# First expert gathered on TensorE, last normed rows stored from ScalarE, two tiles of the last stage summed by TensorE

## The chip, the cores and the metric

One Trainium2 chip, one of its cores; the program runs on that core alone. The metric is device time in microseconds (us), the median of several executions, lower is better. The core has TensorE (PE), VectorE (DVE), ScalarE (ACT), GpSimd (POOL) and SyncE (SP), each with its own instruction stream, and 16 DMA engines that all queues share. Engines wait for one another through semaphores only.

## What is computed

The block has one layer, 512 tokens of width 1024, all in float32. Two mixers, a gated merge and a cross-attention add to the residual `x`; the part that matters here comes after them:

```python
h = rmsnorm(x, norm_ffn_g)                      # 512 x 1024
group_prob = softmax(h @ w_group_router + b_group_router)      # 4 groups
gp, gi = top_k(group_prob, 1)
in_group = logits of the 8 experts of group gi  # h @ w_expert_router + b
ew, ei = top_k(softmax(in_group), 2)            # two experts per token
weights = gp * ew / sum(ew)
for e in range(32):
    hid = silu(h @ w_exp_gate[e]) * (h @ w_exp_up[e])     # 1024 -> 256
    out += combine[:, e] * (hid @ w_exp_down[e])          # 256 -> 1024
x = x + out
return rmsnorm(x, norm_final_g)
```

Each expert has 3 MB of weights, 96 MB in all.

## The kernel before

The tokens lie in four tiles (`NT = 4`) of 128 rows; the residual is `xres[:, t, :]`. Up to the router the work is a list of jobs that `job_order` (L126) writes out by hand; every engine walks the same list and does its part of each job. TensorE does the job and increments `done`, then the engine that `emptied_by` (L205) names reads the job's PSUM bank. Banks are given in turn, eight of them (L290 to L301). The jobs that end the list:

- `("co", t, n)`: half n of the cross-attention's output rows of tile t. VectorE adds it to `xres` (L1865). After n = 1 ScalarE squares the row to get its sum (L1545) and GpSimd makes the inverse root in six small operations (L870 to L875, `ffn_rstd`).
- `("hT", "ffn", t, q)`: TensorE transposes four blocks of `xres` (L1024), ScalarE copies them to `x_turned` (L1548). It waits until both halves of `co` are added.
- `("rt", t)`: router logits, 8 sums (L977 through `sums`), then a chain of some fifteen small operations on VectorE (L1872 to L1888) that picks the two experts. ScalarE makes the normed row `x_row[t]` (L1552, recorded at L1360), and GpSimd, after its own three operations (L880, L882), stores it to `h_rows` in device memory (L884).
- `("pos", t)`: the place of each token within its expert, as two one-hot tables `at_slot` of 128 tokens by 64 slots (L1891, L1894).
- `("ls",)`: the list of rows for each expert, by 32 matmuls (L1269), read by VectorE at L1896 to L1898 (`idx_ready`); `("most",)`: the largest count.

The order of these jobs for the last tile is at L183 and L184.

The expert stage comes next. `UNROLL = 6` sets of weights lie in SBUF, the sixth in the place of the ring. The first six experts are loaded ahead: SP issues five parts of 1 MB and the final norm's gain row after the last `co` job (L747 to L752). From expert 6 on, `load_expert` (L754) loads gate and up when the gate_up of the expert six before is done (L761), and down when its down is done (L763). GpSimd gathers an expert's rows from `h_rows` (L902), after all four stores have landed and the list is there (L886 to L888); up to three gathers are ahead. TensorE turns the rows (L1292), VectorE multiplies them by the norm's gains into `xgT` (L1926), TensorE does gate_up (L1305), then the turn of the next expert, then the hidden layer's transpose (L1326) and down (L1315). ScalarE copies the result (L1569) and GpSimd scatters it to `y_half` (L907). All engines run the 32 experts as a loop over six at a time; on TensorE and VectorE the loop starts at expert 0.

The last stage: after all scatters SP loads the two results of each token (L786, eight loads of 0.5 MB), VectorE adds them to `xres` with their weights, tile by tile (L1955), ScalarE squares (L1593), VectorE makes the inverse root by a shift and three Newton steps (`rms`, L1616). Tiles 0 and 1 are scaled by ScalarE (L1597) and multiplied by the gain row on GpSimd (L967), tiles 2 and 3 by VectorE (L1965). SP stores each tile (L789).

Of the kernel before, what the change touches and what calls it, by code (L numbers as in the profile page):

```python
# [33 lines left out]
P = 128  # L34
# [91 lines left out]
def job_order():  # L126
# [56 lines left out]
    jobs += [("co", 3, 0), ("rt", 2), ("pos", 1), ("co", 3, 1), ("pos", 2), ("hT", "ffn", 3, 0), ("hT", "ffn", 3, 1), ("rt", 3), ("pos", 3)]  # L183
    jobs += [("ls",), ("most",)]  # L184
# [5 lines left out]
PARTIAL = ("gp", "wp")  # L190
# [14 lines left out]
def emptied_by(job):  # L205

    if job[0] in PARTIAL:
        return None
    return "act" if job[0] in ON_ACT or job[:2] == ("hT", "ffn") else "dve"

# [31 lines left out]
def program(nc, x, mem, rel_bias_table, norm_mix_g, w_in, a_sink, b_conv_w, b_A_log, b_dt_bias, b_norm_g,  # L242
# [48 lines left out]
    for n, job in enumerate(jobs):  # L291
        gates = at["gp", 0, 0] <= n <= at["ga", 7]
        if job[0] in ("gp", "ga"):
            bank_index[job] = BANKS - 1
        elif job[0] == "wo":
            bank_index[job] = bank_index["wp", job[1], job[2]]
        else:
            turn_no = (turn_no + 1) % (BANKS - 1 if gates else BANKS)
            bank_index[job] = turn_no
        before_in_bank[job] = held.get(bank_index[job])  # L300
        held[bank_index[job]] = job  # L301
# [6 lines left out]
    with ExitStack() as ctx:  # L308
# [82 lines left out]
        prob = [r.rearrange("p (h m) -> p h m", h=X_HEADS) for r in x_row]  # L391
        x_turned = [r.rearrange("p (k t) -> p k t", k=KD) for r in x_row]
# [48 lines left out]
        at_slot = [cut(NT * CAP, "p (t s) -> p t s", t=NT) for _ in range(2)]  # L441
        dest_of = [cut(NT * EXPERTS, "p (t e) -> p t e", t=NT) for _ in range(2)]
# [36 lines left out]
        hrow_out = [sem("hrow_out0"), sem("hrow_out1")]  # L479
# [35 lines left out]
        put_set, y_in = sem("put_set"), [sem(f"y_in{t}") for t in range(NT)]  # L515

        more_w, more_idx_in, more_idx, more_gathered = sem("more_w"), sem("more_idx_in"), sem("more_idx"), sem("more_gathered")
        more_turned, more_turned_sb, more_gu, more_gth = sem("more_turned"), sem("more_turned_sb"), sem("more_gu"), sem("more_gth")
        more_gated, more_hid, more_hidT, more_hidT_sb = sem("more_gated"), sem("more_hid"), sem("more_hidT"), sem("more_hidT_sb")
        more_down, more_y, more_out = sem("more_down"), sem("more_y"), sem("more_out")  # L520
        fin_ready, out_done = sem("fin_ready"), sem("out_done")
        scale_ready, scaled, early_fin = sem("scale_ready"), sem("scaled"), sem("early_fin")
# [126 lines left out]

        def y_total(b):  # L650
# [40 lines left out]
        def _(sp):  # L691
# [60 lines left out]
            sp.dma_start(gain_out, norm_final_g.rearrange("(o d) -> o d", o=1).to_broadcast([P, D])).then_inc(gains_in, 16)  # L752
# [18 lines left out]
            with sp.If(most > CAP):  # L771
# [8 lines left out]
                sp.wait_ge(more_out, 16 * MORE)  # L780
            for b in range(DEEP):
# [5 lines left out]
            for t in range(NT):  # L787
                sp.wait_ge(*((early_fin, t + 1) if t < 2 else (fin_ready, t - 1)))
# [5 lines left out]
        def _(pool):  # L794
# [28 lines left out]
            for job in jobs:  # L823
# [42 lines left out]
                if k == "co" and c == 1:  # L866
# [8 lines left out]
                    after(pool.tensor_tensor(y, y, y2, ALU.mult), ffn_rstd)  # L875
                if k == "rt":
# [6 lines left out]
                    pool.wait_ge(hrow_ready, c + 1)  # L883
                    pool.dma_start(h_rows[c * P:(c + 1) * P, :], x_row[c]).then_inc(hrow_out[c % 2], 16)  # L884
# [11 lines left out]
            def gather(i, b):  # L896
# [3 lines left out]
                pool.wait_ge(idx_set, i * UNROLL + b + 1)  # L900
                pool.sem_inc(gathering, 1)
# [62 lines left out]
            for t in range(2):  # L964
                pool.wait_ge(scaled, t + 1)
                pool.wait_ge(gains_in, 16)
# [1019 lines left out]
```

## Time and profile before

| | us |
|---|---|
| median of 3 runs | 888.8 (888.28 to 889.62) |
| profiled execution, its own time | 885.0 |
| its span, first to last instruction | 883.1 |
| mean granted TensorE clock | 0.957 of full |
| PE busy / DVE / ACT / POOL | 770.2 / 359.8 / 244.3 / 294.4 |
| moved by DMA | 162.84 MB, 184 GB/s mean |

All durations in the following come from the profiled execution, in which time 0 is the first instruction. A line of a timeline has start, duration, engine, source line, operation, the tiles written and read, the count, and in brackets the engine's idle time before it with what released it. PEld is TensorE's loading of the stationary operand, SPq and POOLq are the issuing of DMAs. [...] An fp32 product is recorded as two matmul records.

### The profile page before, as it was taken

The page shows a single profiled execution, that of the slowest core. Times are in us where ns is not written, and L with a number is a line of the kernel's source. Part 1 is how long each engine was busy: PE and PEld are TensorE (multiplying, and loading weights), DVE is VectorE, ACT ScalarE, POOL GpSimd, SP SyncE. Part 2 cuts the span into 40 slices and gives each one's busy share as a digit, 9 for nine tenths or more (in the row PEclk, how much of TensorE's full clock was granted, in tenths as well). Part 3 has the DMA queues.
Part 4 walks back from the last instruction along what each step waited for, and adds up shares of the span by engine and source line. Part 5 has one row for each costly group of instructions (what it writes and reads, how often), then busy time and mean ns, then how long its engine had stood idle before and what let it go on. Part 6 is the DMA issues. An engine that isn't in the chain of part 4 may idle for free.

```text
span 883.1 us, 14710 instructions
## 1 busy us (share of the span) xinstructions
PE 770.2 (87%) x5715; PEld 631.0 (71%) x5715; DVE 359.8 (41%) x767; ACT 244.3 (28%) x421; POOL 294.4 (33%) x256
## 2 busy tenths in 40 slices
PE   5999999899899979999996998957999999987830
PEld 5888798788788857788885877845777777756610
DVE  6478760562763861236513513551121212121117
ACT  4333242112212746522213446320111111101012
POOL 3823444422530243034442434323333333322102
PEclk9999999999999989999997999967999999999975
DMA  9755504202220431374492455384999999999943
GB/s 256 138 102 108 111 10 96 48 5 46 49 48 2 98 94 36 62 193 94 95 283 50 102 187 212 144 333 173 394 392 392 398 388 390 386 389 389 368 164 153
DMA packets 71513, 162.84 MB, mean 184 GB/s; under 512 B 18876, under 2 KB 44300, under 8 KB 63272
## 3 DMA queue, kind: packets, MB, share of 16 engines
q1 hardware_dynamic: 63920, 150.66, 53.5%
q0 software_dynamic: 5696, 10.50, 3.5%
q10 hardware_dynamic: 1848, 1.02, 0.7%
q8 instruction: 31, 0.51, 0.2%
q14 instruction: 18, 0.15, 0.1%
HBM read 157.57 MB, written 13.04 MB: 193 GB/s over the span
## 4 chain that ended last, share of the span: by engine, by line
PE 54%; DMA 25%; DVE 9%; issue 5%; ACT 4%; POOL 2%; SPq 1%; DVEq 0%; POOLq 0%; ACTq 0%
PE bank L977 14%; DMA arena<-in_w_exp_up 13%; PE bank L984 11%; PE bank L986 10%; PE bank L985 10%; DMA ring<-in_w_exp_up 8%; PE bank L1305 3%; DMA ring<-in_w_cq 1%; PE bank L1315 1%; DVE xres L1955 1%; DVE arena L1664 1%; DMA arena<-y_half 1%; PE bank L1187 1%; DMA h_rows<-hT 1%; ACT w_high L1360 1%
## 5 line engine op out<-in xcount | busy, mean ns | idle before, releaser
L984 PE MATMUL bank<-h_hi,w_high 128*128 128x512 f32 x296 | 123.2, 416 | 2.3 <-DVEq L543 2.0
L807 POOL TENSOR_TENSOR ring_low<-ring,w_high 128x2048 fp32r<-128x2048 f32 (+1 forms) x16 | 71.6, 4477 | 149.5 <-ACT w_high L1360 132.9
L1305 PEld LDWEIGHTS bank<-arena,hT 128*64 128x64 f32 x1728 | 99.7, 139 | 25.4 <-issue 21.5
L985 PE MATMUL bank<-h_lo,w_high 128*128 128x512 f32 x296 | 116.5, 394 | 0.0
L1305 PE MATMUL bank<-arena,hT 128*64 128x128 f32 x1728 | 103.6, 279 | 8.2 <-DMA arena<-in_w_exp_up 7.4
L807 POOL TENSOR_TENSOR w_low<-ring,w_high 128x2048 fp32r<-128x2048 f32 x14 | 64.4, 4599 | 78.9 <-ACT w_high L1360 77.0
L1928 DVE SCALAR_TENSOR_TENSOR rt<-rt,bank 128x128 f32<-128x128 f32 x32 | 9.2, 288 | 181.7 <-ACT rt L1565 181.7
L1360 ACT ACTIVATE w_high<-ring 128x2048 fp32r<-128x2048 f32 (+1 forms) x32 | 58.8, 1838 | 66.6 <-PE bank L986 30.7
L984 PEld LDWEIGHTS bank<-h_hi,w_high 128*128 128x128 f32 x296 | 56.3, 190 | 15.2 <-DVEq L543 2.3
L986 PE MATMUL bank<-h_hi,ring_low 128*128 128x512 f32 x168 | 66.7, 397 | 0.0
L985 PEld LDWEIGHTS bank<-h_lo,w_high 128*128 128x128 f32 x296 | 56.2, 190 | 9.6
L1315 PE MATMUL bank<-arena,rt 128*64 128x512 f32 x216 | 52.3, 605 | 10.3 <-DVE rt L1932 10.3
L907 POOL DMA_INDIRECT y_half<-rows,cst x32 | 32.5, 1015 | 79.2 <-ACT rows L1569 79.2
L984 PE MATMUL bank<-w_high,h_hi 128*128 128x512 f32 (+1 forms) x144 | 51.8, 360 | 1.5 <-ACT w_high L1360 1.5
L986 PE MATMUL bank<-w_high,h_lo 128*128 128x512 f32 (+1 forms) x144 | 51.0, 354 | 0.0
L986 PE MATMUL bank<-h_hi,w_low 128*128 128x512 f32 x128 | 50.0, 390 | 0.0
L1569 ACT ACTIVATE rows<-bank 128x512 f32<-128x512 f32 x32 | 19.1, 597 | 109.2 <-PE bank L1315 109.2
L985 PE MATMUL bank<-w_low,h_hi 128*128 128x512 f32 (+1 forms) x128 | 44.7, 350 | 0.0
L1292 PE MATMUL bank<-cst,hT 64*128 64x64 f32 x256 | 35.0, 278 | 9.5 <-DMA hT<-h_rows,rt 9.5
L1565 ACT ACTIVATE rt<-bank 128x128 f32<-128x128 f32 x32 | 8.9, 277 | 118.8 <-PE bank L1305 118.8
L1292 PEld LDWEIGHTS bank<-cst,hT 64*128 64x128 f32 x256 | 30.6, 200 | 14.9 <-issue 14.9
L902 POOL DMA_INDIRECT hT<-h_rows,rt x32 | 31.1, 973 | 25.3 <-POOL rt L899 25.3
(281 smaller groups left out, 1373.1 us busy)
## 6 DMA issues: line engine op xcount, KB each, us to landing
arena<-in_w_exp_gate SPq DMA_DIRECT2D x27, 1024.0 KB, 11.9
arena<-in_w_exp_up SPq DMA_DIRECT2D x27, 1024.0 KB, 16.9
arena<-in_w_exp_down SPq DMA_DIRECT2D x27, 1024.0 KB, 19.5
ring<-in_w_in SPq DMA_DIRECT2D x33, 512.0 KB, 6.6
ring<-in_w_exp_gate SPq DMA_DIRECT2D x5, 1024.0 KB, 12.9
ring<-in_w_exp_up SPq DMA_DIRECT2D x5, 1024.0 KB, 16.9
ring<-in_w_exp_down SPq DMA_DIRECT2D x5, 1024.0 KB, 19.7
xres<-in_x SPq DMA_DIRECT2D x8, 512.0 KB, 7.1
```

Of the source, the lines that this page charges most:

```text
L807: after(pool.tensor_tensor(low, full, high, ALU.subtract), w_lo)
L902: pool.indirect_dma_start(out=xg[:, b % DEEP, :], out_offset=None, in_=h_rows, in_offset=bass.IndirectOffsetOnAxis(ap=idx[b][0:CAP, :], ax ...
L907: pool.indirect_dma_start(out=y_half, out_offset=bass.IndirectOffsetOnAxis(ap=at_y, axis=0), in_=ysb[:, y, :], in_offset=None, bounds_chec ...
L977: ins = pe.matmul(o, l, r, start=(n == 0), stop=(n == len(pairs) - 1))
L984: pe.matmul(o, l_hi, r_hi, start=(n == 0), stop=False)
L985: pe.matmul(o, l_hi, r_lo, start=False, stop=False)
L986: ins = pe.matmul(o, l_lo, r_hi, start=False, stop=(n == count - 1))
L1292: ins = pe.transpose(bank[:, 0, CAP * kk:CAP * kk + CAP], src, ident[0:CAP, 0:CAP])
L1305: ins = pe.matmul(bank[CAP * half:CAP * half + CAP, 1, P * n:P * n + P], xgT[:, x, kk, :], w[:, kk, P * half:P * half + P], start=(kk == 0 ...
L1315: ins = pe.matmul(bank[CAP * half:CAP * half + CAP, o, :], hidT[:, CAP * kk:CAP * kk + CAP], down[:, kk, 512 * half:512 * half + 512], sta ...
L1360: after(nc.scalar.activation(o, i, ACT.Copy, scale=scale), s)
L1569: nc.scalar.activation(ysb[:, y, :], bank[:, 4 + b % 2, :], ACT.Copy).then_inc(y_sb, 1)
```

## The change

1. **Order of the last jobs.** `pos` 1 goes ahead of `rt` 2; the first transposes of tile 3 go between the two halves of its `co` and wait only for their own half; new jobs `("g0", t)` are placed among the rest. The last transposes (`LAST_TURN`) are copied by VectorE and not by ScalarE.
2. **First expert.** A one-hot table `first_at` of 128 tokens by 64 slots, for expert 0 alone, is made by three GpSimd operations per tile for tiles 0 to 2, and by two VectorE operations for tile 3. Job `g0` multiplies each tile's normed rows by it, 8 fp32 products per tile, summed over the tiles in one PSUM bank: the result is what the turn of the gathered rows gave. The first gather is dropped. In expert 0 the turn of expert 1 comes after down.
3. **Last normed rows.** ScalarE makes tile 3's normed rows in `rows` (before: `x_row[3]`) as soon as the inverse root is there, and issues the store from its own queue. GpSimd still issues those of tiles 0 to 2.
4. **Filling products**, whose result nobody reads, stand before `pos` 3 (three, 256 columns), after the list (two) and in the last stage (four, 512 columns).
5. **First six experts outside the loop** on TensorE and VectorE; the loop starts at turn 1.
6. **Last stage.** The gain row is loaded behind the last expert's weights. Tiles go in the order 2, 0, 3, 1, and each half of a tile's results has its own semaphore. Tiles 2 and 3 are summed in PSUM by TensorE, as identity times `xres` and a diagonal of weights times each result; tiles 0 and 1 by VectorE as before. One power operation on GpSimd and three small VectorE operations replace the shift and the three Newton steps. VectorE does the last product of all four tiles.

```diff
-    jobs += [("co", 3, 0), ("rt", 2), ("pos", 1), ("co", 3, 1), ("pos", 2), ("hT", "ffn", 3, 0), ("hT", "ffn", 3, 1), ("rt", 3), ("pos", 3)]
-    jobs += [("ls",), ("most",)]
+    jobs += [("co", 3, 0), ("pos", 1), ("rt", 2), ("hT", "ffn", 3, 0), ("co", 3, 1), ("g0", 0), ("hT", "ffn", 3, 1), ("pos", 2), ("rt", 3)]
+    jobs += [("g0", 1), ("pos", 3), ("g0", 2), ("ls",), ("g0", 3), ("most",)]
...
+LATE_BANKS = {"g0": 0, "ls": 6, "most": 3}
+FILL = {("pos", NT - 1): 3, "turned": 2}
+LAST_TURN = ("hT", "ffn", NT - 1, 1)
...
+        normed_row = x_row[0:NT - 1] + [rows[:, 1, :]]
...
             for b in range(DEEP):
                 sp.wait_ge(y_out[b], y_total(b))
-            for t in range(NT):
+            for t in LAST_ORDER:
                 for j in range(2):
-                    sp.dma_start(arena[:, (2 * t + j) * D:(2 * t + j + 1) * D], y_of_tile[t, :, j, :]).then_inc(y_in[t], 16)
+                    sp.dma_start(y_rows(t, j), y_of_tile[t, :, j, :]).then_inc(y_in[t][j], 16)
...
+                if k == "pos" and c < NT - 1:
+                    pool.wait_ge(list_ready, c + 1)
+                    job_done(pool, ("xv", NT - 2))
+                    after(pool.tensor_scalar(first_at[:, c, :], at_slot[0][:, c, :], oh[0][:, c, 0:1], None, ALU.mult))
+                    after(pool.tensor_scalar(second_at, at_slot[1][:, c, :], oh[1][:, c, 0:1], None, ALU.mult))
+                    after(pool.tensor_tensor(first_at[:, c, :], first_at[:, c, :], second_at, ALU.add), first_slots)
...
             for b in range(2):
-                pool.wait_ge(hrow_out[b], 16 * NT // 2)
+                pool.wait_ge(hrow_out[b], hrow_total[b])
+            pool.wait_ge(last_hrow_out, 16)
             pool.wait_ge(idx_ready, 1)
+            job_done(pool, ("g0", NT - 2))
...
                     if phase == "ffn":
-                        job_empty(pe, ("co", t, 1))
+                        job_empty(pe, ("co", t, q))
...
+                if k == "g0":
+                    t = job[1]
+                    pe.wait_ge(*((first_slots, t + 1) if t < NT - 1 else (last_slots, 1)))
+                    pe.wait_ge(hrow_ready, t + 1)
+                    for kk in range(KD):
+                        ins = pe.matmul(o[:, CAP * kk:CAP * kk + CAP], normed_row[t].rearrange("p (d k) -> p k d", k=KD)[:, kk, :], first_at[:, t, :],
+                                        start=(t == 0 and kk == 0), stop=(t == NT - 1), skip_group_check=True)
+                    return ins
...
+            pe.wait_ge(weights_ready, 1)
+            for t in (2, 3):
+                for half in range(2):
+                    pe.matmul(sum_banks(t)[:, half, :], ident, xres[:, t, 512 * half:512 * half + 512], start=True, stop=False)
+            for _ in range(4):
+                pe.matmul(bank[:, 3, :], ident, cst[:, 0:512], start=True, stop=True)
+            for t in (2, 3):
+                for j in range(2):
+                    pe.wait_ge(y_in[t][j], 16)
+                    for half in range(2):
+                        ins = pe.matmul(sum_banks(t)[:, half, :], y_weight[j][:, t - 2, :], y_rows(t, j)[:, 512 * half:512 * half + 512], start=False, stop=(j == 1))
+                ins.then_inc(summed, 1)
...
+                    if t == NT - 1:
+                        act.wait_ge(ffn_rstd, NT)
+                        copy(normed_row[t], xres[:, t, :], hrow_ready, scale=rstd[:, 10 + t:11 + t])
+                        act.dma_start(h_rows[t * P:(t + 1) * P, :], normed_row[t]).then_inc(last_hrow_out, 16)
...
+            def roots(a, b):
+                n = slice(14 + a, 14 + b)
+                v, y, y2 = var[:, a:b], rstd[:, n], newton[:, a:b]
+                dve.wait_ge(squared, 14 + b)
+                after(ts(v, squares[:, n], 1.0 / D, EPS, ALU.mult, ALU.add), var_ready)
+                dve.wait_ge(root_ready, b // 2)
+                after(tt(y2, y, y, ALU.mult))
+                after(stt(out=y2, in0=y2, scalar=-0.5, in1=v, op0=ALU.mult, op1=ALU.mult))
+                after(stt(out=y, in0=y2, scalar=1.5, in1=y, op0=ALU.add, op1=ALU.mult))
...
-            for t in range(2):
-                add(t)
-            add(2)
-            rms(14, 2, scale_ready)
-            add(3)
-            rms(16, 2)
...
+            add(0)
+            roots(0, 2)
+            add(1)
+            finish(0, 2)
+            roots(2, 4)
+            finish(2, 4)
```

## Rows read from the trace of the kernel before

**Rows 1.** Stretches: length, busy PE, PEld, DVE, ACT, POOL; clock, DMA share, GB/s

```profile
592.00:594.00 2.00, 0.00 (x0) 0.00 (x0) 1.58 (x10) 0.42 (x2) 0.00 (x0) 0.50 1.02 418
596.00:609.00 13.00, 7.13 (x80) 6.75 (x80) 1.17 (x3) 0.28 (x1) 4.67 (x8) 0.63 0.17 46
609.00:835.00 226.00, 205.56 (x2401) 154.47 (x2402) 43.79 (x119) 25.95 (x59) 68.82 (x117) 0.99 1.02 389
```

**Rows 2.** SP's queue: first weight load behind expert 0, then loads and stores of the last stage

```profile
608.22 0.36 SPq L761 DMA_DIRECT2D arena<-in_w_exp_gate  x1
...
852.35 4.46 SPq L786 DMA_DIRECT2D arena<-y_half  x8
...
871.96 8.46 SPq L789 DMA_DIRECT2D result<-xres  x4
```

**Rows 3.** Chain of waits from the last store of rows to the first expert

```profile
589.84 5.97 DMA h_rows<-hT
...
597.15 3.69 DMA hT<-h_rows,rt
...
601.08 1.13 PE bank L1292 x8
602.23 0.70 DVE hT L1926
602.98 5.09 PE bank L1305 x64
...
609.86 1.94 PE bank L1315 x8
611.80 3.54 PE bank L1305 x64
```

**Rows 4.** Timeline of TensorE over the last jobs (router 2, router 3, list)

```profile
571.53 1.87 PE L977 MATMUL bank<-rt,hT 128*128 128x36 f32 x16
...
581.44 3.27 PE L977 MATMUL bank<-rt,hT 128*128 128x36 f32 x16 [1.44 <-ACT hT L1360]
...
589.00 2.00 PE L1269 MATMUL bank<-cst 128*64 128x32 f32 x32
```

**Rows 5.** Timeline of VectorE over the same stretch

```profile
573.55 0.22 DVE L1872 SCALAR_TENSOR_TENSOR rt<-bank,tiny,rt 128x4 f32<-128x4 f32 x1 [0.38 <-PE bank L977]
...
578.10 0.69 DVE L1865 TENSOR_TENSOR xres<-xres,bank 128x512 f32<-128x512 f32 x1
...
587.68 0.25 DVE L1887 SCALAR_TENSOR_TENSOR rt<-cst,rt 128x32 f32<-128x32 f32 x1
...
589.75 0.54 DVE L1894 TENSOR_SCALAR cst<-rt 128x64 f32<-128x64 f32 x2
```

**Rows 6.** Same columns as rows 1: clock after it fell, and after the last expert

```profile
582.00:583.00 1.00, 1.00 (x6) 1.00 (x7) 0.00 (x0) 0.00 (x0) 0.07 (x1) 0.50 0.83 303
850.00:851.00 1.00, 0.00 (x0) 0.00 (x0) 0.00 (x0) 0.00 (x0) 0.59 (x1) 1.00 0.00 0
```

**Rows 7.** Loads of the stationary operand in the turn of expert 1 (eight)

```profile
607.98 0.96 PEld L1292 LDWEIGHTS bank<-cst,hT 64*128 64x128 f32 x8 [0.17 <-issue]
```

**Rows 8.** Timeline of GpSimd: last operation of tile 3's inverse root

```profile
581.88 0.19 POOL L875 TENSOR_TENSOR tiny<-tiny 128x1 f32<-128x1 f32 x1
```

**Rows 9.** DMA issues, whole span: KB each, median us to landing; and one queue's packets, 560 to 640

```profile
arena<-in_w_exp_down SPq DMA_DIRECT2D x27, 1024.0 KB, 19.5
...
q8 instruction: 5, 0.08, 0.4%
```

**Rows 10.** Timeline of the last stage

```profile
857.53 2.60 DVE L1955 SCALAR_TENSOR_TENSOR xres<-arena,rt,xres 128x1024 f32<-128x1024 f32 x2 [11.34 <-DMA arena<-y_half]
...
868.30 4.72 DVE L1955 SCALAR_TENSOR_TENSOR xres<-arena,rt,xres 128x1024 f32<-128x1024 f32 x2
...
869.59 5.64 POOL L967 TENSOR_TENSOR xres<-xres,arena 128x1024 f32<-128x1024 f32 x2 [19.00 <-ACT xres L1597]
...
877.46 2.61 DVE L1965 SCALAR_TENSOR_TENSOR xres<-xres,tiny,arena 128x1024 f32<-128x1024 f32 x2
```

More of the change, by code:

```diff
@@ L1250, in emit @@
                     t = job[1]
-                    job_empty(pe, ("hT", "ffn", t, 1))
+                    for q in range(2):
+                        job_empty(pe, ("hT", "ffn", t, q))
                     if t == 0:
@@ L1281, in _ @@
                     continue
+                for _ in range(FILL.get(job, 0)):
+                    pe.matmul(bank_of(job)[:, 0:256], ident, cst[:, 0:256], start=True, stop=True)
                 emit(job if job[0] != "sc" else ("sc", job[1], job[2] - 2)).then_inc(done, 1)
+            spare = jobs[-BANKS]
+            job_empty(pe, spare)
+            for _ in range(FILL["turned"]):
+                pe.matmul(bank_of(spare)[:, 0:256], ident, cst[:, 0:256], start=True, stop=True)
             for job in held.values():
-                job_empty(pe, job)
+                if job[0] not in LATE_BANKS:
+                    job_empty(pe, job)
             def turn(b, s):
@@ L1295, in turn_rows @@
             def turn_rows(i, b):
-                pe.wait_ge(gathered[b], 16 * i + 16)
+                pe.wait_ge(gathered[b], 16 * i + (16 if b else 0))
                 turn(b, turned)
@@ L1330, in expert @@
                 down_rows(b, 4 + b % 2, down_done)
-            turn_rows(0, 0)
-            with pe.Fori(0, TURNS, 1) as i:
+                if turn_last:
+                    turn_next()
+            pe.sem_inc(turning, 1)
+            job_done(pe, ("g0", NT - 1))
+            pe.sem_inc(turned, 1)
+            for b in range(UNROLL):
+                expert(0, b, lambda: turn_rows((b + 1) // UNROLL, (b + 1) % UNROLL), turn_last=(b == 0))
+            with pe.Fori(1, TURNS, 1) as i:
                 for b in range(UNROLL):
@@ L1590, in _ @@
                 act.wait_ge(y_out[b], y_total(b))
[L1591 to L1597 removed]
+            for n, t in enumerate(LAST_ORDER):
+                act.wait_ge(*((summed, t - 1) if t >= 2 else (res_ready, t + 1)))
+                source = sum_banks(t) if t >= 2 else xres[:, t, :].rearrange("p (h c) -> p h c", h=2)
+                junk = rows[:, n % 2, :].rearrange("p (h c) -> p h c", h=2)
+                after(nc.scalar.activation(junk, source, ACT.Square, accum_out=squares[:, 14 + n:15 + n]), squared)
         @block.vector
@@ new lines, in finish @@
+            def finish(a, b):
+                for place in range(a, b):
+                    t = LAST_ORDER[place]
+                    halves = lambda tile: tile.rearrange("p (h c) -> p h c", h=2)
+                    source = sum_banks(t) if t >= 2 else halves(xres[:, t, :])
+                    after(stt(out=halves(xres[:, t, :]), in0=source, scalar=rstd[:, 14 + place:15 + place], in1=halves(gain_out), op0=ALU.mult, op1=ALU.mult), fin_ready)
+            for j, t in itertools.product(range(2), (2, 3)):
+                ins = ts(y_weight[j][:, t - 2, :], ident, wgt[j][:, t:t + 1], None, ALU.mult)
+                after(ins, weights_ready if (j, t) == (1, 3) else step["dve"])
```

119 lines of the change are left out of this document (73 added, 46 removed).

## The prediction

> **What bounds the kernel now.** I read the stretches first, then the chain of waits backwards, then the timelines of the engines that the chain names. From 609 to 835 us the DMA engines are full (share 1.02, 389 GB/s) and TensorE is not [rows 1]: the weights of the last 26 experts set the pace, some 8.9 us each. In the 13 us before, the share is 0.17 [rows 1]. The first six experts are loaded ahead, that load ends at about 595, and the stream goes on only when expert 0 has read its gate and up weights: SP issues at 608.22 [rows 2]. So whatever brings expert 0's gate_up forward brings the whole stream forward, as long as the loads ahead are done, which 418 GB/s up to 594 and next to nothing after 596 show [rows 1]. [...] Behind the stream comes a last stage of loads, sums and norms from 852.35 to 883.1.
>
> **Front of the stage, step by step.** All in the old trace's time.
>
> *Order and last transposes.* On VectorE the four operations of `pos` 1 ran between router 2 and the last add, about 1.15 us; now they fill the 0.38 us that it waited before router 2 [rows 5] and push router 2 instead. The add that started at 578.10 starts at about 577.8 and ends at 578.5. TensorE has `g0` 0 in front of the last transposes. An fp32 product is two records, so `g0` is 16 loads of a strided 128-column operand; eight such loads took 0.96 us [rows 7], so 1.92. A bound below is the turn's 1.13 in all [rows 3], one above 3.27, the 16 records of router 3 at the lower clock [rows 4]. I take 1.92, the row with the same operand. The last half of `co` ended at 576.7 and now has 0.5 us of transposes ahead of it, so about 577.1; then 577.1 + 1.9 = 579.0, transposes until 579.6, VectorE's copy 0.7 (as the gains, from PSUM, [rows 3]), router 3 at 580.5 against 581.44. Before, ScalarE did the square and two copies in front of it. Router 3 took 3.27 us at the lower clock and router 2 1.87 at the upper [rows 4]. With `g0` and the filling products TensorE has no gap over about 1 us here, so I take 1.87: it ends at 582.4, 2.3 us earlier. The inverse root ended at 582.07 [rows 8] and moves by 0.3 at most, so it does not become the wait. VectorE's chain takes the same 3.1 us: the choice that came at 587.93 [rows 5] comes at 585.6.
>
> *Up to gate_up.* `g0` 1 and three filling products (some 1.3 us) lie in TensorE's wait for that choice and cost nothing; without that cover they would cost their 1.3. `pos` 3 ends at 586.2; its tables on VectorE, old end 590.29 [rows 5], at 587.5, and the two new `first_at` operations at 588.1, beside `g0` 2, which ends at 588.2. The list took 2.00 us at the lower clock [rows 4]; half of it at the upper gives 589.2. `g0` 3 ends at 591.2, the gains take 0.7, gate_up starts at 591.95 against 602.98, **11.0 earlier**, and at the upper clock takes 3.55: done at 595.5 against 608.07, **12.6 earlier**. GpSimd's nine new operations for tiles 0 to 2 lie in waits of tens of us of that engine and hold nobody while the root is in time.
>
> *Expert 1.* ScalarE stores the last rows after the root (582.1) and one copy of 1.15, from about 583.5. With GpSimd's 5.97 [rows 3] it lands at 589.5. The gather landed 5.0 us behind the store (595.8 to 600.8) [rows 3]; so the rows are there at 594.5. Expert 0's down ended at 611.80 [rows 3], 3.7 us after gate_up, so now at 599.2, and only then does TensorE turn expert 1. The store may land as late as 594.2 for nothing. What is late next is the turn itself: it no longer lies under expert 0's hidden layer, so gate_up 1 is done at 599.2 + 1.1 + 0.8 + 3.5 = 604.6. The loads for expert 6 flow from about 596.6 (data came 1 us behind the issue), need 3.15 MB / 389 GB/s = 8.1 us and end at 604.7; the next flow at 605.6. **The stream idles some 1.0 us**, so it moves by 12.6 - 1.0 = **11.6 us**. The gain row (0.5 MB, 1.3 us) is now behind the last weights, where the old trace has a DMA share under 0.3, and is wanted only 12 us later: nothing.
>
> ScalarE's store shares the 16 DMA engines with 5 MB of weights. [...] No run here shows ScalarE's queue under such a load; one in plain order behind the weights is the third case below.
>
> **Last stage**, still in old time. Its start moves with the stream. Before: adds from 857.53, a slow add (4.72 us for two, where two took 2.60) beside GpSimd's 5.64 us of products, last products from 877.46 to 880.07, last store until 883.1 [rows 10, 2]. After: tile 2's results are there at 857.4 (as tile 0's were), then each tile's 1.05 MB takes 2.6 us: tile 0 at 860.1, tile 3 at 862.6, tile 1 at 864.2. TensorE's identity products (four at about 0.9 us: down's four half-width ones took 1.94, two full ones' worth [rows 3]) and four filling ones run from 848.3 to 855.5, under the loads. With a fast clock tile 2 is summed at 859.3 and squared at 860.5; VectorE's sum of tile 0 ends at 861.9, its square at 863.2. Roots: 0.2, GpSimd 0.9 (single power operation and hops), 0.6: 865.0. Tile 1's sum 2.6: 867.7. Two products of 1.3: 870.3. Roots again 1.7: 872.0. Two products: 874.6. Store 3.0: 877.6. Gain 883.1 - 877.6 = **5.5 us**. TensorE's tile 3 is wanted only at 870, so a low clock there costs nothing.
>
> **Sum.** 885.0 - 11.6 - 5.5 = 867.9 for an execution like the profiled one. The median of the runs shown is 3.8 above it (888.8), so 888.8 - 17.1 = **871.7 us**.
>
> **Rivals.**
> - *The clock stays low up to expert 0 (0.13).* TensorE still waits in small gaps, and before the change it fell with gaps of 1.6 and 1.4 us. Then router 3 costs 1.4 more, the list 1.0, `g0` 2 and 3 1.4 each, `pos` 0.4, gate_up 1.5: 7.1 in all, 878.8. For the last stage 1.00 at 850 without work [rows 6] speaks against it. [...]
> - *The last rows land late (0.08).* If the store waits behind the weights, the longest median landing in the trace is 19.5 us [rows 9]: lands at 603.0, gathered at 608.0, gate_up 1 done at 613.4 against 604.6: 8.8 later, 880.5. The stream would have a hole and TensorE a wait in front of L1292.
> - *The last stage gains nothing (0.08).* Identity and filling products at the lower clock are 14 us instead of 7, and the sums follow late: only 11.6 stay, 877.2.
> - *The change does not move the stream (0.04)*, because the loads ahead or something else hold it: only 5.5 stays, 883.3. Against it stand the 13 us of empty DMA [rows 1].
> - *Slower: code fetch (0.03).* TensorE and VectorE now have six experts outside the loop, more code just where the stream begins. Instruction fetches run on the same DMA engines (5 packets between 560 and 640 [rows 9]). One that waits behind the weights for 19.5 us, in front of expert 1, while nothing is asked for, takes back all: 888.8 - 17.1 + 19.5 = 891.2. It decides from 17.1 us on; shorter ones only eat gain. Against it: no such stall in the long straight code before 560.
>
> **How the numbers follow.** The forecast has 0.62; a mixture that ends near no change 0.02. The likeliest case gives 871.7; with `g0` at its lower bound and no idle of the stream it is about 869, and the runs scatter by 1.3, so the range starts at 868. It reaches to 879, which takes in the low clock and the last stage's failure. A measurement of this kernel can tell about 0.2% (1.8 us) from no change. Faster 0.94, within it 0.03, slower 0.03.
>
> **What would show it.** Right: gate_up of expert 0 near 592 and 3.5 us long, SP's first load behind it near 595.7, ScalarE's store landing before 594, the end of the weights near 829, the last stage about 25 us from its first load to the end instead of 30.8. Wrong: a granted clock of 0.50 after 583, a wait for the gather in front of L1292 in expert 0, or a DMA share below 0.9 after 600.

## Result, and the profile after

| | before | after |
|---|---|---|
| median, beside each other (6 runs each) | 888.04 us | 883.06 us (880.39 to 885.34) |
| ratio, 95% interval | | 0.9939 (0.9919 to 0.9959) |
| profiled execution, its span | 885.0, 883.1 us | 883.49, 881.7 us |

The change makes the kernel 5.0 us faster, where 17.1 were forecast, and 883.06 lies outside the range of 868 to 879. The two profiled executions differ by less than the medians do, and one part of that lies outside the change: in code that nothing touched, the new one loses 1.8 us between 136 and 304 us and is 2.1 us late at 560, and everything behind is read with that offset of 2.1.

SP's queue says which of the three terms failed. The view is its timeline in the kernel after, at the places of [rows 2]; the columns are start, duration, engine, line, operation (SPq's records are SP's DMA issues, DMA_DIRECT2D).

```profile
611.23 0.36 SPq L788 DMA_DIRECT2D arena<-in_w_exp_gate  x1
...
620.69 0.34 SPq L788 DMA_DIRECT2D arena<-in_w_exp_gate  x1
...
856.26 4.54 SPq L814 DMA_DIRECT2D arena<-y_half  x8
...
872.97 6.00 SPq L817 DMA_DIRECT2D result<-xres  x4
```

- **Last stage.** From its first load to the end of the span 881.7 - 856.26 = 25.4 us, against 30.75. It gains 5.3; 5.5 were forecast.
- **The stream.** From the first load behind expert 0 to the last stage's loads 245.0 us, against 852.35 - 608.22 = 244.1. It is 0.9 longer; the forecast had 1.0, for the serial turn of expert 1. That the turn is the cause isn't shown: in the kernels below that have no serial turn the same stretch takes 244.0 to 245.2.
- **The front.** The first load comes at 611.23 against 608.22: 3.0 later, 0.9 without the offset. It was to come 12.6 earlier. The miss is here: 13.5 us.

The chain of waits of the kernel after through that front (start, duration, what; the stretch that [rows 3] and [rows 4] showed before):

```profile
579.16 3.63 PE bank L1316 x16
582.79 0.46 PE bank L1062 x4
...
583.34 0.70 DVE hT L1762
...
584.17 3.60 PE bank L1015 x16
587.77 3.83 PE bank L1316 x16
591.61 2.67 PE bank L1330 x6
594.27 0.47 PE bank L1015 x4
594.74 3.87 PE bank L1316 x16
598.61 1.85 PE bank L1308 x32
600.47 4.00 PE bank L1316 x16
...
604.84 1.87 PE bank L1336 x4
606.71 4.37 PE bank L1359 x64
```

L1316 is `g0` (eight fp32 products, recorded as x16), L1062 the last transposes, L1015 router 3 and then `pos` 3, L1330 and L1336 the filling products, L1308 the list, L1359 gate_up of expert 0. Before, this chain ran over a round trip, the store (5.97 us), the gather (3.69) and their waits, and then over a gate_up of 5.09 us where expert 1's took 3.54 [rows 3]; now it is TensorE from end to end. The round trip has gone, and the work put in its place takes as long. Each `g0` takes 3.6 to 4.0 us where 1.92 was reckoned, and the filling products stand in the chain, where they were to be hidden.

The stretches of the kernel after, with the columns of [rows 1], show the clock. Taken one us at a time from 580 to 612, 28 of the 32 are at 1.00 or 0.50 and four between (0.56, 0.82, 0.89, 0.99); the upper and the lower clock are these two here.

```profile
582.00:584.00 2.00, 1.60 (x12) 1.49 (x11) 0.66 (x1) 0.00 (x0) 1.56 (x6) 1.00 1.04 416
584.00:586.00 2.00, 1.82 (x9) 1.85 (x9) 0.93 (x7) 1.15 (x1) 0.74 (x3) 0.53 1.00 324
586.00:594.00 8.00, 8.00 (x31) 7.53 (x31) 2.83 (x15) 0.00 (x0) 1.64 (x5) 0.50 1.00 412
594.00:596.00 2.00, 2.00 (x11) 1.93 (x10) 0.90 (x6) 0.00 (x0) 0.00 (x0) 0.91 1.01 416
596.00:598.00 2.00, 2.00 (x10) 2.00 (x10) 0.54 (x2) 0.00 (x0) 0.00 (x0) 0.94 0.30 121
598.00:604.00 6.00, 6.00 (x50) 5.82 (x50) 0.61 (x3) 0.00 (x0) 1.64 (x4) 0.50 0.00 0
608.00:610.00 2.00, 2.00 (x40) 2.00 (x38) 0.27 (x2) 0.00 (x0) 0.00 (x0) 1.00 0.26 70
```

The first `g0` (579.16 to 582.79) ran at a granted clock of 1.00 and took 3.63 us all the same: its length isn't the clock's doing. The clock falls at 584 (0.56 from 584 to 585, then 0.50), a little after that `g0` and just behind a gap of 0.58 us before router 3. It comes back between 594 and 598 and falls a second time, and this time TensorE had counted as busy in every microsecond since 585; what brought the second fall isn't shown. From 598 to 604 the DMA engines move nothing at all: the stream waits for this chain, as before.

The last stage went by the forecast's steps. The timeline of VectorE in the kernel after, where [rows 10] had a sum of 4.72 us and a wait for GpSimd's products:

```profile
863.38 2.60 DVE L2047 SCALAR_TENSOR_TENSOR xres<-arena,rt,xres 128x1024 f32<-128x1024 f32 x2 [11.17 <-DMA arena<-y_half]
...
869.02 2.60 DVE L2047 SCALAR_TENSOR_TENSOR xres<-arena,rt,xres 128x1024 f32<-128x1024 f32 x2
...
877.32 1.28 DVE L2067 SCALAR_TENSOR_TENSOR xres<-xres,tiny,arena 128x1024 f32<-128x1024 f32 x1
```

VectorE has two sums instead of four, each pair of operations at 2.60, waits for no product of GpSimd's, and is done at 877.32 + 1.28 = 878.6, 3.1 us before the span's end, as before.

### The profile page after: what moved, and what is told of

Its sections match the earlier page's. It is cut to its first block, busy times and chain, and to the rows that moved or that the text cites. A ratio compares the mean times of both kernels' runs of the same rounds, so it can differ in the third digit from the quotient of the medians.

```text
span 881.7 us, 14886 instructions
## 1 busy us (share of the span) xinstructions
PE 803.0 (91%) x5813; PEld 654.9 (74%) x5813; DVE 354.5 (40%) x756; ACT 241.3 (27%) x418; POOL 292.3 (33%) x263
## 3 DMA queue, kind: packets, MB, share of 16 engines
q10 hardware_dynamic: 1992, 1.55, 0.8%
## 4 chain that ended last, share of the span: by engine, by line
PE 59%; DMA 22%; DVE 8%; issue 4%; ACT 3%; POOL 2%; SPq 1%; DVEq 0%; POOLq 0%; ACTq 0%
PE bank L1015 15%; DMA arena<-in_w_exp_up 12%; PE bank L1022 11%; PE bank L1024 11%; PE bank L1023 10%; DMA ring<-in_w_exp_up 8%; PE bank L1359 4%; PE bank L1369 2%; PE bank L1316 2%; DMA ring<-in_w_cq 1%; DVE arena L1749 1%; PE bank L1346 1%; PE bank L1225 1%; DMA arena<-y_half 1%; ACT w_high L1434 1%
## 5 line engine op out<-in xcount | busy, mean ns | idle before, releaser
L1359 PEld LDWEIGHTS bank<-arena,hT 128*64 128x64 f32 x1728 | 97.5, 137 | 24.5 <-issue 24.5
L1359 PE MATMUL bank<-arena,hT 128*64 128x128 f32 x1728 | 101.2, 275 | 7.8 <-DMA arena<-in_w_exp_up 6.9
L1024 PEld LDWEIGHTS bank<-h_hi,ring_low 128*128 128x128 f32 x168 | 32.3, 192 | 7.7
L1434 ACT ACTIVATE arena<-bank 128x512 f32<-128x512 f32 (+1 forms) x39 | 23.3, 597 | 47.3 <-PE bank L1024 32.0
```

Source lines behind the costliest of these rows:

```text
L1024: ins = pe.matmul(o, l_lo, r_hi, start=False, stop=(n == count - 1))
L1359: ins = pe.matmul(bank[CAP * half:CAP * half + CAP, 1, P * n:P * n + P], xgT[:, x, kk, :], w[:, kk, P * half:P * half + P], start=(kk == 0 ...
L1434: after(nc.scalar.activation(o, i, ACT.Copy, scale=scale), s)
```

## The experiments

Each median stands beside runs of the kernel before on the same chip, and the ratio is to those. The kernels ran on several chips, on which the kernel before took 887.87 to 889.17 us, so two of them are compared by their ratios as well. A trace is of one execution; how late it is in the code that nothing touched differs too (0.3 us early to 3.9 late at 560, against the kernel before). Kernels without a word on it differ from the kernel after in the lines shown alone.

### The layout of the normed rows

The operand of `g0` is every eighth element of a row (`p (d k) -> p k d`, 32 bytes apart). This kernel stores the normed rows block by block, so that `g0` and the turns read neighbouring elements; ScalarE's copies now read with the stride.

```diff
+by_k = lambda r: r.rearrange("p (k d) -> p k d", k=KD)
+by_d = lambda r: r.rearrange("p (d k) -> p k d", k=KD)
-copy(normed_row[t], xres[:, t, :], hrow_ready, scale=...)      # and the same for x_row[c]
+copy(by_k(normed_row[t]), by_d(xres[:, t, :]), hrow_ready, scale=...)
-ins = pe.matmul(o[...], normed_row[t].rearrange("p (d k) -> p k d", k=KD)[:, kk, :], first_at[:, t, :], ...)
+ins = pe.matmul(o[...], by_k(normed_row[t])[:, kk, :], first_at[:, t, :], ...)
-src = xg[:, b % DEEP, :].rearrange("p (d k) -> p k d", k=KD)[:, kk, :]
+src = by_k(xg[:, b % DEEP, :])[:, kk, :]
```

> The changed kernel with the normed rows stored block by block (k, then d), so that TensorE reads the stationary operand of every g0 product and of every turn without a stride; the result is the same. Theory A (the strided stationary loads make g0 3.8 us where I counted 1.9, and a TensorE fed that slowly lets its clock fall): a g0 takes about 1.9 us, the clock stays at its upper level longer, expert 0's gate_up starts some 8 to 10 us earlier, total 872 to 876 us. Theory B (the stride costs nothing, the clock falls anyhow): g0 stays at 3.6 us or more at the lower clock, total 881 to 884.

Measured: 873.09 us (872.07 to 874.45), ratio 0.9827 (0.9799 to 0.9855). First the loads of the first `g0`'s stationary operand, in the kernel after and then in this one (timeline of PEld, whose records are LDWEIGHTS, the loads of that operand; both at clock 1.00):

```profile
578.76 3.89 PEld L1316 LDWEIGHTS bank<-rows,hT 128*128 128x128 f32 x16
```

```profile
577.10 1.98 PEld L1318 LDWEIGHTS bank<-rows,hT 128*128 128x128 f32 x16
```

The same sixteen loads, 0.24 us each with the stride and 0.12 without. Then TensorE's timeline of this kernel:

```profile
577.32 1.89 PE L1318 MATMUL bank<-rows,hT 128*128 128x64 f32 x16
...
580.77 2.08 PE L1017 MATMUL bank<-rt,hT 128*128 128x36 f32 x16 [0.58 <-DVE hT L1764]
582.66 3.65 PE L1318 MATMUL bank<-rows,hT 128*128 128x64 f32 x16
586.11 2.87 PE L1332 MATMUL bank<-cst 128*128 128x256 f32 x6
...
589.38 1.98 PE L1318 MATMUL bank<-rows,hT 128*128 128x64 f32 x16
...
592.34 2.00 PE L1318 MATMUL bank<-rows 128*128 128x64 f32 x16
...
595.41 3.77 PE L1361 MATMUL bank<-arena,hT 128*64 128x128 f32 x64
```

Router 3 is back at 2.08 us, gate_up at 3.77. `g0` 1 and the filling products behind it are long, and the clock says why: 0.61 of full between 582 and 584 and 0.50 until 588, then up again. So the term's 1.92 was right for an operand in one piece, and the layout made it 3.8.

ScalarE pays for the stride now, in the copy of the last rows (its timeline; 1.15 us in the kernel after):

```profile
582.75 2.20 ACT L1436 ACTIVATE rows<-xres,tiny 128x1024 f32<-128x1024 f32 x1 [2.46 <-POOL tiny L905]
```

The stride is eight elements, and both engines take about double with it: 0.24 against 0.12 us a load on TensorE, 2.20 against 1.15 us for the copy on ScalarE. No run here tries a stride between one and eight elements, so from which stride on it costs isn't shown.

### The index of `g0` alone

To part the gain of `g0`'s loads from that of the turns (0.7 us instead of 1.1 above), this kernel changes one index. Expert 0 then gets its inputs in another order of the width, so that its products are of other pairs; nothing else differs.

```diff
-normed_row[t].rearrange("p (d k) -> p k d", k=KD)[:, kk, :]
+normed_row[t].rearrange("p (k d) -> p k d", k=KD)[:, kk, :]
```

> The changed kernel with one index changed: g0 reads its stationary blocks from the normed rows without a stride, while the rows, the gather and the turns stay as they are. Expert 0 then gets its 1024 inputs in another order, so its result is another one; the work is the same. Theory A (all of the gain of the block-wise rows lies in g0's loads): a g0 takes 1.9 us at the upper clock, total 872 to 875 us. Theory B (part of it came from the turns of the other 31 experts, which went from 1.09 to 0.71 us): 876 to 880.

Measured: 872.85 us (872.67 to 873.35), ratio 0.9817 (0.9801 to 0.9833). It equals the kernel above: the whole gain of some 10 us comes from the loads of the four `g0`. The shorter turns bring no net gain, and the stream behind expert 0 is no shorter with them (245.9 us above, 245.8 here).

### No filling products

```diff
-FILL = {("pos", NT - 1): 3, "turned": 2}
+FILL = {"turned": 0}
```

> The changed kernel without the filling products ahead of pos 3 and behind the list. Theory A (they run at the lower clock, 2.7 and 1.9 us, and stand in the path, since g0 has already eaten the wait they were to lie in): 3 to 4 us faster than the changed kernel, 879 to 880. Theory B (they pay by the clock they keep up for the first gate_up): gate_up of expert 0 is 5.1 instead of 4.4 us and the list slower, total the same, 882 to 884.

Measured: 879.60 us (876.38 to 882.60), ratio 0.9883 (0.9850 to 0.9916), 3.5 less than the kernel after, whose interval begins (0.9919) where this one has ended. With strided loads the filling products do harm. The last row of TensorE's front in this kernel:

```profile
603.66 6.19 PE L1359 MATMUL bank<-arena,hT 128*64 128x128 f32 x64 [0.50 <-DVE hT L1713]
```

They bought something, 4.42 us instead of 6.19 for this gate_up, and cost more: 2.4 in the step before `g0` 2 (7.00 against 4.65 from the start of `g0` 1) and 1.3 before gate_up. In the traces that makes the front 1.9 us longer (32.1 against 30.2); the rest of the 3.5 isn't found there. The same edit on the block-by-block layout:

> The kernel with block-wise rows, without the filling products. Theory A (with the short g0 the filling pays, since it brings the clock back up before g0 2, the list, g0 3 and gate_up): those stay at the lower clock (3.6, 2.0, 3.6 and 5.1 us where they took 2.0, 1.1, 2.0 and 3.8), less 2.4 and 1.1 us of filling, total 874 to 877. Theory B (filling is in the path as it was with the strided loads): 870 to 872.

Measured: 875.31 us (874.49 to 878.52), ratio 0.9842 (0.9825 to 0.9859), 2.2 more than with them (2.5 more than the kernel with the one index changed, which ran on the same chip, and whose slowest run is faster than the fastest here). The granted clock is at 0.50 from 586 to 604, `g0` 2 and 3 take 3.65 and 3.68, gate_up 6.53. In the traces the front takes 26.3 us without the filling products and 21.9 with them, though there they stood in the chain as well (the step of `g0` 1 takes 6.72 us against 4.37): the clock came back behind them, and the list, gate_up and both `g0` were shorter by 6.9 in sum. So they don't pay by lying in a wait. They pay by what a faster clock gives the work behind them, and a strided `g0` takes about the same at either level (3.63 us at a granted clock of 1.00, 3.83 at 0.50), so that in the kernel after only gate_up gained.

### The first expert gathered again

The kernel after without part 2 and its filling products; order, ScalarE's store, the six experts outside the loop and the last stage stay.

```diff
-... ("co", 3, 1), ("g0", 0), ("hT", "ffn", 3, 1), ("pos", 2), ("rt", 3)]
-jobs += [("g0", 1), ("pos", 3), ("g0", 2), ("ls",), ("g0", 3), ("most",)]
+... ("co", 3, 1), ("hT", "ffn", 3, 1), ("pos", 2), ("rt", 3)]
+jobs += [("pos", 3), ("ls",), ("most",)]
...
-            job_done(pe, ("g0", NT - 1))
-            pe.sem_inc(turned, 1)
+            turn_rows(0, 0)
```

> The changed kernel with its second part undone: no one-hot products and no filling, the first expert's rows gathered as before; order of jobs, ScalarE's store, six experts outside the loop and the last stage stay. Theory A (the store leaves 4 us earlier and the gather follows the list): expert 0's gate_up starts 3 to 5 us earlier than in the kernel before, total 878 to 880, faster than the changed kernel, so g0 as built costs more than the round trip that it spares. Theory B (g0 still gains): total 884 or more.

Measured: 877.84 us (877.10 to 880.01), ratio 0.9878 (0.9847 to 0.9910): 5.2 faster than the kernel after. Most of that is the filling: against the kernel without it (879.60, ratio 0.9883) this one is 1.8 faster, with intervals that overlap, though in the traces its first load behind expert 0 comes 3.0 us earlier (607.02 against 610.01). As built, the products spare nothing, and together with their filling they cost more than the round trip. TensorE's wait for that round trip in this kernel:

```profile
599.37 1.12 PE L1337 MATMUL bank<-cst,hT 64*128 64x64 f32 x8 [7.50 <-DMA hT<-h_rows,rt]
```

The same with the block-by-block layout, to see what short products are worth:

> The block-by-block layout of the normed rows, with the first expert gathered as before the change and no filling products; order, ScalarE's store, the unrolled six and the last stage stay. It tells what the first expert by products is worth once its loads are short. Theory A (the products are right, only their loads were slow): here expert 0 waits for the round trip, and the strided copy of the last rows by ScalarE, 1.1 us longer, lies in it, while each turn is 0.4 us shorter; SP's first load behind expert 0 comes near 607.7, 8 us after that of the kernel with short products, and the median is 877 to 880. Theory B (the gain of the block-by-block layout is its shorter turns, in every expert, and the products are worth nothing): the median is 873 to 875, and the stream's own pace, first load to first load of the last stage, is shorter than in the kernel with the change.

Measured: 880.28 us (875.98 to 880.98), ratio 0.9895 (0.9859 to 0.9931); first load at 607.12, stream 851.15 - 607.12 = 244.0, no shorter than before. It is a trifle above theory A's 877 to 880 and far from B. Against 873.09 the products with short loads are worth 7.2 us by the medians and 6 by the ratios, filling included. Part of that lies elsewhere: this trace's last stage takes 27.7 us where the other's takes 25.0. VectorE's sum of tile 1 starts 1.6 us later in it, waiting for results, and TensorE's sum of tile 3, 6.44 us at a granted clock of 0.50 (862 to 868) instead of 3.70 at 1.00, then holds the last norms, where the forecast had it that a low clock costs nothing. The first load comes 7.7 us later than in the other trace, of which 0.8 were lost ahead of 560, and the stream takes 1.9 less, which leaves the products some 5 us. The idea of part 2 was right, its layout wrong.

### The last stage alone

The kernel before with parts 5 and 6: new last stage, late gain row, six experts outside the loop.

```diff
-# the kernel before
+LAST_ORDER, roots, finish, summing products and the load of the gain row as in the kernel after
+TensorE and VectorE: for b in range(UNROLL): expert(0, b, ...), and the loop from turn 1
```

> The kernel before with the new last stage, the gain row loaded late and six experts outside the loop, and nothing else. Theory A (the last stage gives its 5.3 us and the front as built loses a little): 882.5 to 883.5, the same as the changed kernel or just under it. Theory B (code outside the loop or the late gain row costs something): over 885.

Measured: 880.92 us (880.20 to 884.04), ratio 0.9924 (0.9896 to 0.9953), a little below theory A's number. Its last stage takes 879.1 - 853.78 = 25.3 us, the first load comes at 608.60 against 608.22. So the last stage alone gives as much as the whole change does (the two ratios can't be told apart), and the code outside the loop holds nobody. The kernel with the first expert gathered again has parts 1 and 3 besides, and is 3.1 us faster than this one (877.84, on the same chip; the intervals overlap): that is about what the new order and ScalarE's store are worth by themselves.

### Holding the clock

In the kernel with the new layout the clock fell between 582 and 584 although TensorE's records leave only one gap there, the 0.58 us before router 3. One filling product is put into that gap:

```diff
-FILL = {("pos", NT - 1): 3, "turned": 2}
+FILL = {("rt", NT - 1): 1, ("pos", NT - 1): 3, "turned": 2}
```

> The kernel with block-wise rows and one more filling product (256 columns, 0.43 us) in TensorE's gap ahead of router 3. Theory A (the clock fell at 583 for want of work in that gap, and this is enough): clock at its upper level throughout, g0 1 takes 1.9 instead of 3.65 us, gate_up starts 2 to 3 us earlier, total 870 to 871. Theory B (the fall does not hang on that gap): same as without it, 873.

Measured: 871.78 us (870.23 to 872.75), ratio 0.9800 (0.9782 to 0.9818). The stretches of this kernel (columns of [rows 1]) and its gate_up:

```profile
582.00:586.00 4.00, 3.94 (x33) 3.56 (x33) 2.38 (x12) 1.54 (x3) 3.15 (x10) 1.00 1.04 414
586.00:590.00 4.00, 3.88 (x29) 3.38 (x28) 2.94 (x17) 1.04 (x1) 1.26 (x4) 1.00 1.00 401
590.00:594.00 4.00, 4.00 (x58) 3.87 (x57) 1.56 (x7) 0.00 (x0) 0.00 (x0) 1.00 1.00 413
594.00:598.00 4.00, 4.00 (x65) 3.64 (x65) 2.67 (x15) 0.42 (x2) 0.99 (x3) 1.00 0.73 294
```

```profile
594.63 3.77 PE L1361 MATMUL bank<-arena,hT 128*64 128x128 f32 x64
```

The granted clock stays at 1.00 until expert 0's gate_up is done (594.63 to 598.4), and the front is 2.9 us shorter than with the new layout alone. The time shows this less clearly: the median is 1.3 us lower, and the intervals overlap. The same with three instead of one, which makes router 3 wait:

> The same with three filling products ahead of router 3, 1.3 us in a gap of 0.6, so 0.7 us late for router 3. Theory A (the clock looks at how much work TensorE gets in this stretch, and three are enough where one may not be): clock at the upper level, gate_up starts 2 us earlier, total 871. Theory B: 0.7 slower than without, 874.

Measured: 873.98 us (871.01 to 875.08), ratio 0.9819 (0.9797 to 0.9842). The granted clock is 1.00 up to gate_up's end here too, and the time isn't better; its interval overlaps the others', so it only says that more of them doesn't help.

### Expert 1's turn, and an earlier list

Two kernels on top of the last but one. First the turn of expert 1 goes between the hidden layer's transpose and down, in expert 0:

```diff
                 pe.transpose(bank[:, 2, 0:P], hid, ident).then_inc(hidT_done, 1)
+                if turn_last:
+                    turn_next()
...
                 down_rows(b, 4 + b % 2, down_done)
-                if turn_last:
-                    turn_next()
```

> The kernel with block-wise rows and one filling product ahead of router 3, and in expert 0 the turn of expert 1 between the hidden layer's transpose and down, no longer behind down. Theory A (the serial turn of expert 1 leaves a hole in the weight stream, as my prediction had it with 1.0 us): gate_up of expert 1 starts 1.2 us earlier and the total is about 1 lower, 870.5 to 871. Theory B (the loads for expert 6 still fill the DMA engines until expert 1 is through): total the same, 871.5 to 872.5.

Measured: 870.33 us (869.88 to 874.10), ratio 0.9812 (0.9787 to 0.9837): the lowest median, but not the lowest ratio (0.9800, of the kernel that it starts from), so no gain is shown. Nor did theory A's step come: from SP's first load behind expert 0 to the start of expert 1's gate_up it takes 602.45 - 595.98 = 6.5 us, against 605.11 - 598.84 = 6.3 without the edit, since the turn now waits 1.16 us for its gather. This trace is 2.6 us shorter than the other because it was 2.8 us ahead at 560, in code that the edit doesn't touch. Then, without that edit, `g0` 2 ahead of `pos` 3, so that TensorE has work while VectorE chooses:

```diff
-jobs += [("g0", 1), ("pos", 3), ("g0", 2), ("ls",), ("g0", 3), ("most",)]
+jobs += [("g0", 1), ("g0", 2), ("pos", 3), ("ls",), ("g0", 3), ("most",)]
...
-FILL = {("rt", NT - 1): 1, ("pos", NT - 1): 3, "turned": 2}
+FILL = {("rt", NT - 1): 1, ("ls",): 2, "turned": 2}
```

> The same kernel (turn behind down) with g0 2 ahead of pos 3, where it lies in TensorE's wait for VectorE, and the three filling products there replaced by two ahead of the list. Theory A (g0 2's 2.0 us come out of the path, VectorE's tables of 1.7 us are the next wait): gate_up of expert 0 starts about 0.5 to 1 us earlier, total 871. Theory B (the gap of 1.2 us behind pos 3 lets the clock fall): list, g0 3 and gate_up slower, 874.

Measured: 873.47 us (872.11 to 874.98), ratio 0.9839 (0.9823 to 0.9856). Gate_up came 0.9 us earlier (593.76), and the time is longer, clear of the 0.9800 without the edit: expert 1's turn waited 1.49 us for its gather and the stream took 247.9 us. The clock held (1.00 to the end of gate_up), so this isn't theory B's cause. Neither theory said so. Both edits together:

> Both edits at once. If both gain it is 870 to 871, the fastest of all; if neither does, it is 871.5 to 873.

Measured: 875.58 us (873.86 to 877.82), ratio 0.9860 (0.9837 to 0.9882), a higher median than either (the interval overlaps that of the second). The chain's DMA steps (store of the last rows, gather of expert 1) in the kernel with the turn moved, then in the kernel with both edits:

```profile
584.25 8.44 DMA h_rows<-rows
...
594.46 3.86 DMA hT<-h_rows,rt
```

```profile
586.11 8.53 DMA h_rows<-rows
...
596.41 8.64 DMA hT<-h_rows,rt
```

In the kernel with `g0` 2 ahead and the turn behind down:

```profile
596.96 5.74 DMA hT<-h_rows,rt
```

And in the kernel with both edits TensorE's wait and the stretch behind it:

```profile
605.19 1.09 PE L1348 MATMUL bank<-cst,hT 64*128 64x64 f32 x8 [7.04 <-DMA hT<-h_rows,rt]
```

```profile
606.00:608.00 2.00, 2.00 (x9) 0.65 (x9) 0.69 (x1) 0.00 (x0) 0.87 (x2) 0.50 0.09 23
```

The gather takes 3.86, 8.64 and 5.74 us. It was issued 1.5 us ahead of SP's load for expert 6 in the first (595.98), 0.4 ahead in the second (596.83) and 0.7 ahead in the third (597.69). With both edits TensorE waits 7.04 us, with down behind that wait, and then the stream has a hole. In all three GpSimd issues the gather late because the last rows' store lands late, 8.2 to 8.5 us after it starts. Once expert 0 is early, this store is the next thing to be late, and an expert 0 that is earlier still only puts the weights beside the gather. That the weights are what slows it is read from these rows, one execution each, and wasn't tried by itself (a kernel that holds the load back until the gather has landed would do it).

## Why the prediction was wrong

TensorE's front step by step, from start to start in its timelines, in us:

| step | forecast | after | new layout | and clock held |
|---|---|---|---|---|
| `g0` 0 | 1.9 | 3.63 | 1.88 | 1.89 |
| transposes, copy, to router 3 | 1.5 | 1.55 | 1.57 | 1.57 |
| router 3 | 1.9 | 3.41 | 1.89 | 1.78 |
| `g0` 1, filling, to the end of `pos` 3 | 3.8 | 7.00 | 6.72 | 3.91 |
| `g0` 2 | 2.0 | 3.96 | 1.91 | 1.91 |
| list | 1.0 | 1.86 | 1.05 | 1.06 |
| `g0` 3 | 2.0 | 3.86 | 1.84 | 1.83 |
| to gate_up | 0.75 | 2.37 | 1.23 | 1.24 |
| gate_up | 3.55 | 4.42 | 3.77 | 3.77 |
| sum | 18.4 | 32.1 | 21.9 | 19.0 |

- **What bounds the kernel: right.** The stream follows expert 0's gate_up, in every kernel here; and in the kernel after the DMA engines stand still ahead of it.
- **The failed step: "`g0` is 16 loads of a strided 128-column operand; eight such loads took 0.96 us, so 1.92."** It measured 3.6 to 4.0. The row chosen [rows 7] has the stride too, and 0.12 us a load, but its operand is 64 partitions high and goes into a transpose; with 128 partitions and an fp32 product the load is 0.24. I called it "the row with the same operand", and it wasn't. Even the upper bound, 3.27, was too low: it came from loads in one piece at the lower clock. The bounds should have been held open because no row showed a strided load of 128 partitions.
- **What hung on it.** "`g0` 1 and three filling products lie in TensorE's wait and cost nothing": with `g0` 1 at 3.83 they don't fit, and 2.67 us of them stood in the chain. The working named that price too low as well ("they would cost their 1.3", at the lower clock it was twice that).
- **The clock: wrong.** "TensorE has no gap over about 1 us here, so I take 1.87." The gaps were small, as forecast, and the clock fell all the same. In the kernel with the new layout it fell behind one gap of 0.58 us, and in the step of `g0` 1 that cost 2.8 us against the last column. With strided loads it was at 0.50 for most of the 24 us from 584 to 608. The rival "the clock stays low" had 0.13 and this as its mechanism. One product or three in the gap kept the granted clock at 1.00 to the end of expert 0's gate_up in all five kernels that have them. That says nothing of the second fall in the kernel after, near 598, where the records show no gap.
- **With both premises put right the forecast's own path comes out**: 19.0 us against 18.4, and 871.78 us against 871.7. That the time agrees so well is luck. Between the two traces the span shrinks by 12.1 us (883.1 to 871.0), or 14.6 with the 2.5 that the second loses ahead of 560, and not by 17.1: 11.9 of the forecast 12.6 for the first load, 5.2 of 5.5 for the last stage, and the stream 2.5 longer (246.6) instead of 1.0, as expert 1's gate_up ran at the lower clock until 608 (5.37 us; 0.50 from 602 on). The medians agree because the trace before was of an execution below the median (885.0, where the runs beside this kernel have 889.17).
- **The last stage: right**, 5.3 for 5.5. The 0.9 us in it for GpSimd's power operation was an estimate that no row of the kernel before shows; VectorE waited 0.93 and 0.95 us for that operation in the kernel after. **The serial turn: not refuted**, 0.9 for 1.0, but kernels without it differ by as much (244.0 to 245.2), and moving the turn gained nothing. With an early front the stream is 1.8 longer (845.28 - 599.39 = 245.9 in the kernel with the new layout).
- **ScalarE's store: a term too small, without effect.** It landed 9.1 us after its issue (585.51), not 5.97. In the kernel after that is covered, since the gather waits for the list until 601.4:

```profile
601.40 0.42 POOL L936 COPY rt<-rt 64x1 int32<-64x1 int32 x2 [8.80 <-DVE cst L1988]
```

 It is not ScalarE's queue that is slow: GpSimd's store of tile 2, issued at 581.61, took 9.4 beside the same weights. That the store would take GpSimd's time was the forecast's estimate. The 5.97 of [rows 3] was of a store at the end of the loads; GpSimd's store of tile 2 in the kernel before, issued at 578.5 beside the weights, had taken 8.4. The term counted once the front was short, in the last three kernels.
- **Code fetch, and the stream not moved: did not happen**, by the last stage alone (880.92) and by the new layout (873.09).

The sum over the profiled executions closes: +3.0 for the first load, +0.9 for the stream, -5.3 for the last stage are -1.4, the difference of the spans. That the medians differ by 5.0 and not by 1.5 is the 2.1 us from untouched code, and some 1.5 that no view of one execution can tell from the scatter of the runs.

## What to carry to other kernels

A stride of eight fp32 elements doubled the time of TensorE's loads here (3.89 against 1.98 us for sixteen) as it nearly did that of ScalarE's copy (2.20 against 1.15): before a product takes a stored array as its weights, look at the stride of each load, and where it is as wide pay for the layout where the array is made. A row of the trace prices a new operation only if type, partitions, stride and clock are the same; where one differs, no bound comes from that row. Filling products pay by what a faster clock gives to the work behind them, less what they add to the chain, so they have to be weighed again whenever work beside them changes; a kernel's trace is compared with another's only after the difference in untouched code is taken off; and after a stage has been moved forward, ask again which transfer must now land first, and what else is issued beside it.

## What the runs showed of the hardware

- Sixteen loads of a 128x128 fp32 operand took 1.98 us with neighbouring elements and 3.89 us with elements 32 bytes apart, both at a granted clock of 1.00. At 0.50 the strided ones took no longer (3.91 in the kernel after), the others 3.53 (block-by-block layout without filling): with the stride the two clocks differ by 0.02 us here, which hides the fall of the clock in these rows.
- The granted clock stayed at 0.50 while TensorE's records covered every microsecond (586 to 594 in the kernel after: busy 8.00 of 8.00), and fell again near 598 with no gap in the records since 585. A busy share near 1 in a profile is no sign that the clock stays up.
- A gather of 64 rows landed after 3.86 us when issued 1.5 us ahead of 2 MB of weight loads, after 5.74 when issued 0.7 us ahead and after 8.64 when issued 0.4 us ahead.
- A store of 0.5 MB beside weight loads landed 8.4 to 9.4 us after its issue on GpSimd's queue (kernels before and after) and 9.1 on ScalarE's (kernel after).

## The kernel to keep

It is the kernel after with the block-by-block layout and one filling product ahead of router 3: 871.78 us, ratio 0.9800 (0.9782 to 0.9818) to the kernel before, and 11.3 us below the kernel after. Expert 1's turn between the hidden layer's transpose and down (870.33, ratio 0.9812) does no harm that can be measured and isn't shown to help.
